# A router joined to the turn ahead of it, with its products per token tile, and the adaptive vectors' weights scaled by ScalarE

## What is computed

```
for layer in range(DEPTH):
    shift_m, scale_m, gate_m, shift_f, scale_f, gate_f = adaln(c, ada_w[layer], ada_b[layer])
    h = rmsnorm(x, norm_mix[layer]) * (1.0 + scale_m) + shift_m
    ...
    h = rmsnorm(x, norm_ffn[layer]) * (1.0 + scale_f) + shift_f
    x = x + gate_f * grouped_moe(h, router_w, router_b, moe_w_gate[layer], moe_w_up[layer], moe_w_down[layer])

def grouped_moe(h, ...):          # 16 experts in 4 groups, 256 tokens
    aff = sigmoid(xf @ router_w)
    biased = (aff + router_b).reshape(T, N_GROUPS, EXPERTS_PER_GROUP)
    grp_score = sum(top_k(biased, 2)); g_sel = argmax(grp_score)
    local = top_k(biased[tok, g_sel], 2)
    w = aff[tok, expert] / sum(...)
    # each token through its two experts (SwiGLU, hidden 512), summed with w
```

## Time and profile before

| | |
|---|---|
| median of 3 runs | 2317.37 us (2312.05 to 2318.6) |
| the profiled execution | 2318.01 us, its span 2316.2 us |
| TensorE, busy | 2108.3 us, 91% of the span |
| VectorE, busy | 1591.7 us, 69% |
| ScalarE, busy | 983.3 us, 42% |
| GpSimd, busy | 709.8 us, 31% |
| mean granted clock of TensorE | 0.937 of full speed |

### The profile page before, as it was taken

How to read it: one execution, slowest core, us unless ns; L and a number is a source line. 1 busy time by engine, 2 the same in 40 slices (tenths; PEclk the granted TensorE clock), 3 DMA queues, 4 the chain that set the end, 5 groups by cost and what they waited for, 6 DMA issues and landing times.

```text
span 2316.2 us, 30766 instructions
## 1 busy us (share of the span) xinstructions
PE 2108.3 (91%) x13090; PEld 1824.9 (79%) x13090; DVE 1591.7 (69%) x1308; ACT 983.3 (42%) x1069; POOL 709.8 (31%) x353
## 2 busy tenths in 40 slices
PE   7998887999899899699989977999998986999997
PEld 6897876999899898699978666877776874877775
DVE  5798536899899774699953556666666247656665
ACT  4433445433433354443333434554453234444553
POOL 2899200899599500089920000000000000000000
PEclk9999898999999899799989987999998787999999
DMA  9886522787678554278754105778986203688874
GB/s 328 272 270 227 183 91 85 261 269 257 230 263 268 174 170 146 95 264 269 246 186 146 55 10 194 278 287 325 341 293 220 82 1 127 226 315 330 310 293 178
DMA packets 224568, 495.95 MB, mean 214 GB/s; under 512 B 11816, under 2 KB 167576, under 8 KB 199696
## 3 DMA queue, kind: packets, MB, share of 16 engines
q1 hardware_dynamic: 200608, 410.20, 51.3%
q0 software_dynamic: 23552, 82.75, 10.4%
q10 hardware_dynamic: 272, 1.05, 0.1%
HBM read 486.57 MB, written 12.10 MB: 215 GB/s over the span
## 4 chain that ended last, share of the span: by engine, by line
PE 82%; DVE 11%; ACT 3%; issue 2%; DMA 2%; DVEq 0%; SPq 0%; ACTq 0%
PE psum L971 79%; DVE nrm L1978 2%; DVE low L1978 2%; DMA ring<-in_ffn_w_up 2%; PE psum L1031 1%; PE psum L1544 1%; PE psum L1198 1%; ACT wh L1633 1%; DVE hl L1978 1%; DVE wide L1978 0%; DVE xl L1978 0%; DVE aux L1978 0%; DVE nrm L2044 0%; DVE nrm L2052 0%; DVE nrm L2042 0%
## 5 line engine op out<-in xcount | busy, mean ns | idle before, releaser
L1978 DVE TENSOR_TENSOR low<-ring,wh 128x2048 fp32r<-128x2048 f32 (+2 forms) x338 | 967.7, 2889 | 350.1 <-ACT wh L1633 349.6
L1633 ACT ACTIVATE wh<-ring 128x2048 fp32r<-128x2048 f32 (+2 forms) x338 | 641.1, 1904 | 616.6 <-PE psum L971 327.1
L971 PE MATMUL psum<-xh,wh 128*128 128x256 f32 x1832 | 521.5, 285 | 8.4 <-DVE low L1978 4.8
L971 PE MATMUL psum<-xl,wh 128*128 128x256 f32 x1832 | 520.3, 284 | 0.0
L971 PE MATMUL psum<-xh,low 128*128 128x256 f32 x1832 | 518.2, 283 | 0.0
L742 POOL TENSOR_TENSOR big<-big 128x1024 f32<-128x1024 f32 x144 | 376.4, 2614 | 11.3
L971 PEld LDWEIGHTS psum<-xh,wh 128*128 128x128 f32 x1832 | 352.7, 193 | 14.2 <-issue 7.9
L971 PEld LDWEIGHTS psum<-xl,wh 128*128 128x128 f32 x1832 | 350.9, 192 | 1.5
L971 PEld LDWEIGHTS psum<-xh,low 128*128 128x128 f32 x1832 | 351.1, 192 | 0.0
L971 PE MATMUL psum<-wh,xh 128*128 128x256 f32 (+5 forms) x864 | 279.0, 323 | 12.5 <-DVEq L645 5.9
L971 PE MATMUL psum<-wh,xl 128*128 128x256 f32 (+5 forms) x864 | 278.2, 322 | 0.0
(11 more groups left out here) (338 smaller groups left out, 2463.4 us busy)
## 6 DMA issues: line engine op xcount, KB each, us to landing
ring<-in_moe_w_gate SPq DMA_DIRECT2D x64, 1024.0 KB, 5.6
ring<-in_moe_w_up SPq DMA_DIRECT2D x64, 1024.0 KB, 6.2
ring<-in_moe_w_down SPq DMA_DIRECT2D x64, 1024.0 KB, 5.8
big<-in_ada_w POOLq DMA_DIRECT2D x48, 1024.0 KB, 7.6
ring<-in_ffn_w_gate SPq DMA_DIRECT2D x44, 1024.0 KB, 5.4
ring<-in_ffn_w_up SPq DMA_DIRECT2D x44, 1024.0 KB, 5.6
ring<-in_ffn_w_down SPq DMA_DIRECT2D x44, 1024.0 KB, 5.9
ring<-in_mlstm_w_in SPq DMA_DIRECT2D x16, 1024.0 KB, 5.6
```

What stands on the lines that cost most here:

```text
L971: return pe.matmul(out_, lhsT, rhs, start=start, stop=stop, **kw)
L1633: act.activation(wh[n % PARTS][:, 0:w], ring[SLOT_OF[n]][:, 0:w], ACT.Copy).then_inc(high, 1)
L1978: return dve.tensor_tensor(out_, a, b, op)
```

## The change

**Adaptive vectors.** ScalarE takes the multiplication by c over: after the down piece's high half of chunks 1 to 8 it waits for the load of one or two pieces (`ADA_PIECES`), and scales each with eight operations of 128x256, one for each column of c (`scale_ada`). GpSimd waits for that (`ada_scaled`) where it waited for the load, and only adds.

**Turn and router.** The pair joins `JOINED`. The router's products are done per token tile: those of tile 0 in the turn, after the wait for the second normed tile and before its transposes, those of tile 1 in the router. ScalarE's copy of the token rows moves into the turn, for tile 0 after its first two copies, for tile 1 after the last two and after a small Sigmoid that brings the table in.

**Ranks and slots.** The comparisons of the three rank computations are two whole operations each instead of eight quarters; one bias addition instead of two; the one-hot of windows 0 and 1 is made first, and the gather of part 0 waits only for it.

**Start of the experts.** The first piece's high and low halves are made right after the first gather copy, and the first expert's gate product waits for the gather copies one by one.

```diff
@@ -228,6 +228,7 @@
         ada_bias_in = sem("ada_bias_in")
+        ada_scaled = sem("ada_scaled")
         ada_step = sem("ada_step")
...
@@ -626,12 +627,13 @@
+        ADA_PIECES = {1: (0,), 2: (1, 2), 3: (3,), 4: (4, 5), 5: (6,), 6: (7, 8), 7: (9,), 8: (10, 11)}
         ADA_TURNS = {0: [(0, 0)], 1: [(0, 3)], 2: [(1, 0)], 3: [(1, 3)]}
         JOINED = [s > 0 and (name, STAGES[s - 1][0]) in (("norm", "residual"), ("final", "residual"),
-                                                         ("turn", "norm"), ("ffn", "turn"), ("project", "turn"), ("moe", "router"),
+                                                         ("turn", "norm"), ("ffn", "turn"), ("project", "turn"), ("moe", "router"), ("router", "turn"),
                                                          ("latent", "project"),
...
@@ -750,17 +752,16 @@
                         pool.wait_ge(ada_out, 16 * (q - 1))
-                    pool.wait_ge(ada_in[j % 2], 32 * q0 + 16 * (j // 2 + 1))
-                    piece, n = ada_w[j % 2], 17 * q + 4 * r
-                    step(n + 1, piece, piece, spread(ccol[:, :], 2, 256), ALU.mult)
-                    step(n + 2, piece[:, 0:4], piece[:, 0:4], piece[:, 4:8], ALU.add)
-                    step(n + 3, piece[:, 0:2], piece[:, 0:2], piece[:, 2:4], ALU.add)
-                    step(n + 4, total[:, 256 * r:256 * r + 256], piece[:, 0], piece[:, 1], ALU.add)
+                    pool.wait_ge(ada_scaled, 4 * q + r + 1)
+                    piece, n = ada_w[j % 2], 13 * q + 3 * r
+                    step(n + 1, piece[:, 0:4], piece[:, 0:4], piece[:, 4:8], ALU.add)
+                    step(n + 2, piece[:, 0:2], piece[:, 0:2], piece[:, 2:4], ALU.add)
+                    step(n + 3, total[:, 256 * r:256 * r + 256], piece[:, 0], piece[:, 1], ALU.add)
                     if j + 2 < rounds:
...
                         pool.wait_ge(ada_bias_in, 16 * (q + 1))
-                        step(17 * q + 17, total[0:1, :], total[0:1, :], ada_bias, ALU.add)
+                        step(13 * q + 13, total[0:1, :], total[0:1, :], ada_bias, ALU.add)
                         pool.dma_start(modpart[layer][first + turn], total).then_inc(ada_out, 16)
...
@@ -1026,10 +1027,22 @@
                         pe.wait_ge(normed, 2 * ran(s, "norm") - 2 + t + 1)
+                    if q == 2 and STAGES[s + 1][0] == "router":
+                        route_products(k, 0)
                     for i in range(4):
...
+            def route_products(turn_, t):
...
+                tokens = slice(t * P, (t + 1) * P)
+                for kt in range(KT):
+                    if kt % 4 == 0:
+                        pe.wait_ge(turn_low, 4 * turn_ + 2 * t + kt // 4 + 1)
+                    last = three(psum[0:E, 0, tokens], both((rw_high, rw_low), slice(0, P), slice(E * kt, E * kt + E)),
+                                 both(xs, slice(0, P), kt, tokens), kt == 0, kt == KT - 1)
+                return last
             def ffn(s, k, chunks):
...
@@ -1396,10 +1409,7 @@
             def router(s, k):
-                for kt in range(KT):
-                    last = three(psum[0:E, 0, 0:T], both((rw_high, rw_low), slice(0, P), slice(E * kt, E * kt + E)),
-                                 both(xs, slice(0, P), kt, slice(0, T)), kt == 0, kt == KT - 1)
-                last.then_inc(route_pe, 1)
+                route_products(ran(s, "turn") - 1, 1).then_inc(route_pe, 1)
                 pe.wait_ge(route_act, k + 1)
...
@@ -1423,7 +1433,7 @@
                     pe.wait_ge(rows_low, 2 * k + 2)
-                    pe.wait_ge(slots_set, 4 * k + 4)
+                pe.wait_ge(slots_set, 6 * k + 2 * part + 2)
                 for j, bank in enumerate(banks):
...
@@ -1439,6 +1449,7 @@
             def weights_of_slots(k):
+                pe.wait_ge(slots_set, 6 * k + 6)
                 for w in range(WINDOWS):
...
@@ -1459,9 +1470,7 @@
                                 if half == 0 and which == "g":
-                                    if q == 0:
-                                        pe.wait_ge(gather_low, 8 * k + 4)
-                                    elif q == 1:
+                                    if q == 1:
                                         pe.wait_ge(gather_low, 8 * k + 8)
...
@@ -1475,6 +1484,8 @@
                                     kt = i + half * KT // 2
+                                    if q == 0 and which == "g" and w == 0 and i % 2 == 0:
+                                        pe.wait_ge(gather_low, 8 * k + kt // 2 + 1)
                                     if w < 4:
...
@@ -1663,6 +1674,16 @@
                                    psum[:, q, :].rearrange("p (a b) -> p a b", a=4), ACT.Copy).then_inc(turn_high, 1)
+                    if STAGES[s + 1][0] == "router" and q % 2:
+                        token_rows(s, q // 2)
...
+            def token_rows(s, t):
...
+                if t == 1:
+                    link(act.activation(stat[:, 7:8], const[:, C_EPS:C_EPS + 1], ACT.Sigmoid))
+                act.wait_ge(normed, 2 * ran(s, "norm") - 2 + t + 1)
+                act.activation(rows_h[:, t, :].rearrange("p (k q) -> p k q", k=KT),
+                               nrm[:, t, :].rearrange("p (q k) -> p k q", k=KT), ACT.Copy).then_inc(rows_high, 1)
             def ffn(s, k, chunks):
...
@@ -1687,7 +1708,18 @@
                         exp_of_pads()
+                    if k in ADA_TURNS:
+                        for j in ADA_PIECES.get(c, ()):
+                            scale_ada(3 * k, j)
                 early_highs(s)
...
+            def scale_ada(q0, j):
...
+                act.wait_ge(ada_in[j % 2], 32 * q0 + 16 * (j // 2 + 1))
+                piece = ada_w[j % 2]
+                for kk in range(KT):
+                    ins = act.activation(piece[:, kk, :], piece[:, kk, :], ACT.Copy, scale=ccol[:, kk:kk + 1])
+                ins.then_inc(ada_scaled, 1)
             def early_highs(s):
@@ -1709,6 +1741,8 @@
                             .then_inc(gather_high, 1)
+                        if part == 0 and j == 0:
+                            high_of(0)
                 def silu_of(q):
...
@@ -1740,7 +1774,7 @@
                 gather_copies(0)
-                for m in range(PARTS):
+                for m in range(1, PARTS):
                     high_of(m)
...
@@ -1934,12 +1968,9 @@
             def router(s, k):
-                for t in range(TT):
-                    act.activation(rows_h[:, t, :].rearrange("p (k q) -> p k q", k=KT),
-                                   nrm[:, t, :].rearrange("p (q k) -> p k q", k=KT), ACT.Copy).then_inc(rows_high, 1)
                 act.wait_ge(route_pe, 3 * k + 1)
                 act.activation(route[0:E, R_AFF:R_AFF + T], psum[0:E, 0, 0:T], ACT.Sigmoid).then_inc(route_act, 1)
-                act.activation(stat[:, 7:8], const[:, C_EPS:C_EPS + 1], ACT.Silu)
+                link(act.activation(stat[:, 7:8], const[:, C_EPS:C_EPS + 1], ACT.Silu))
             def final(s, k):
...
@@ -2139,6 +2170,8 @@
                            hi[:, to, :].bitcast(F32), ALU.subtract).then_inc(gather_low, 1)
+                        if part == 0 and j == 0:
+                            low_of(0)
                 def weighted_hidden(q):
...
@@ -2179,7 +2212,6 @@
                 gather_rests(0)
-                low_of(0)
                 dve.wait_ge(slot_weights, k + 1)
...
@@ -2591,17 +2623,15 @@
                 affinity = psum[:, 1, 0:2 * E].rearrange("p (a b) -> p a b", b=4)
-                rb = small[:, S_RB:S_RB + E].rearrange("p (g e) -> p g e", g=4)
-                for t in range(TT):
-                    link(tt(biased_[:, 4 * t:4 * t + 4], affinity[:, 4 * t:4 * t + 4], rb, ALU.add))
+                link(tt(route[:, 64:96].rearrange("p (t e) -> p t e", t=TT),
+                        psum[:, 1, 0:2 * E].rearrange("p (t e) -> p t e", t=TT),
+                        spread(small[:, S_RB:S_RB + E], 1, TT), ALU.add))
                 def ranks(values, n, g_, e_, out_):
-                    for j in range(4):
-                        other = spread(values[:, :, j], 2, 4)
-                        tt(g_[:, :, j, :], values, other, ALU.is_gt)
-                        last = tt(e_[:, :, j, :], values, other, ALU.is_equal)
-                    link(last)
+                    mine, other = spread(values, 2, 4), spread(values, 3, 4)
+                    tt(g_, mine, other, ALU.is_gt)
+                    link(tt(e_, mine, other, ALU.is_equal))
                     link(tt(e_, e_, spread(lower, 1, n), ALU.mult))
...
@@ -2648,9 +2678,11 @@
                                               in1=spread(seat, 2, WINDOWS), op0=ALU.mult, op1=ALU.add))
+                for w in (0, 2):
+                    for t in range(TT):
+                        tt(onehot[:, t, w:w + 2], spread(iota, 1, 2), spread(seats[:, t, w:w + 2], 2, P), ALU.is_equal)\
+                            .then_inc(slots_set, 1)
                 for t in range(TT):
```

(2 more changed lines are left out.)

## The result

The changed kernel takes 2292.37 us (median of four runs, 2292.11 to 2296.82), beside 2316.98 for the kernel before (four runs). The ratio is 0.9909, with an interval of 0.9883 to 0.9935: 24.6 us less, where 18.5 were forecast. The time lies in the range given, and 1 us outside the sum of the forecast's own bounds (23.6 us gained).

A forecast was written before the change was run, and what follows sets the result against it. TensorE was taken to bound the kernel, waiting only in the first FFN stage and the routers. Gains of 12.1 us there and 6.4 us for both routers, 18.5 in all, took 2317.4 to about 2299 us; range 2291 to 2311.

The forecast's parts named there:

- The bound: Whole kernel: TensorE carries it, waiting only in the first FFN stage (12.5 us for low halves) and in the routers.
- The end of the first FFN stage: First FFN stage and residual: relieving GpSimd gains 12.1 us, bounds nothing and 15 us.
- The wait of 6.1 us: End of first FFN stage: TensorE's wait for low halves goes, as GpSimd is idle from about 199 us; 6.1 us.
- Rival (2): First FFN stage: GpSimd's end moves less, the 6.1 and 3.8 us stay, 2309 us; chance 0.11.
- VectorE's lateness at the residual: Behind the first FFN stage: residual started at 228.0 though ScalarE's root was there at 226.0; 1.9 us go.
- the slow product of x and the gain: Behind the first FFN stage: this product took 3.11 us instead of 1.22; 1.9 us go.
- The early wait of 2.24 us: Earlier in the first FFN stage: TensorE's wait follows a hidden rest that GpSimd stretched; 2.2 us go.
- rival (1): FFN stages: ScalarE's queue becomes the bound, late gate high halves stall TensorE in 16 two-piece chunks; 2331 us, chance 0.12.
- Cost zero in all four stages: FFN stages: ScalarE's new load waits cost TensorE nothing, the gate's high half coming up to 5 us later being covered.
- ScalarE's scaling: FFN stages: eight 128x256 operations take 2.6 us a piece (2.5 to 3.4), some 125 us in all.
- The router: Both routers: scores 2.2 us later, experts 1.8 us earlier, clock 1.4 us; 3.2 us gained each, 6.4 for both.
- rival (3): Routers: 128-token products cost as much as 256-token ones or more, no clock gained; about 2308 us, chance 0.14.

The follow-up runs named there:

- ada_first: The kernel before with ScalarE scaling the adaptive weights in the first FFN stage alone, GpSimd multiplying in the other three, router as before: 2304.37 us, ratio 0.9947.
- nojoin: The changed kernel with the turn-router join undone: 24 products on 256 tokens and the rows' copies behind the turn, as before; 2289.34 us, ratio 0.989.
- no_ranks: The changed kernel with the ranks' eight quarter comparisons back in place of the whole ones: 2297.62 us in one run.
- ada_only: The kernel before with the adaptive vectors' part alone (ScalarE scales, GpSimd only adds), router as before: 2301.34 us, ratio 0.9928.

## Why the prediction was right, step by step

**The bound** was read rightly in the main: FFN 1 and 2 gave nothing (ada_first), the first FFN stage and the routers gave nearly the whole. That the fourth stage repeats the second's row was not quite so: a window over 181 us of it in the kernel before has TensorE idle for 0.9 us.

```profile
985.50:1166.50 181.00, 180.13 (x1284) 168.71 (x1283) 173.62 (x66) 67.79 (x47) 164.19 (x66) 1.00 0.79 261
```

That was worth about 0.8 us, which the sum has at nothing.

**The end of the first FFN stage**, forecast 12.1 us. By the start of the first norm's scaling (237.74 us before, 223.04 after), 14.7 us are gained. The terms:
- The wait of 6.1 us is gone, with GpSimd done at 196.1 us (forecast 199) and the cast at 0.43 us. As forecast. Rival (2) is out.
- VectorE's lateness at the residual is gone (2.1 us, counted from the end of the down products; forecast 1.9), and so is the slow product of x and the gain (3.11 to 1.22, 1.9). As forecast.
- I missed two terms. Behind the 6.1 us of idle time the last down products of the kernel before ran at the low clock:

```profile
219.80:223.20 3.40, 3.35 (x8) 2.71 (x9) 3.40 (x2) 0.00 (x0) 3.32 (x2) 0.50 0.03 10
```

  Eight products there took what sixteen take in the changed kernel (209.80 to 213.20, granted clock 1.00). Over the 24 products behind the wait this was 1.8 us: they lag the same products of the changed kernel by 8.0 us at their first and by 9.8 at their last. I took the clock into account behind the router's wait and forgot it here. And the two updates of x at the residual took 1.92 and 1.66 us instead of 1.28: 1.0 us more, the same disturbance by GpSimd in two rows that I had not looked at.
- The early wait of 2.24 us at 88.59 is gone, but a new one took its place:

```profile
93.65 0.36 PE L972 MATMUL psum<-xh,wh 128*128 128x256 f32 x1 [2.30 <-DVE low L2009]
```

  Ahead of it the queues of ScalarE and GpSimd, and VectorE's from 89.4 to 93.4 us, show why:

```profile
84.32 3.31 ACT L1721 ACTIVATE big<-big,ccol 128x256 f32<-128x256 f32 x8 [2.86 <-DMA big<-in_ada_w]
87.54 3.71 ACT L1644 ACTIVATE wh<-ring 128x2048 fp32r<-128x2048 f32 x2
```
```profile
88.92 8.48 POOL L744 TENSOR_TENSOR big<-big 128x1024 f32<-128x1024 f32 x3
```
```profile
89.47 4.03 DVE L2009 TENSOR_TENSOR low<-ring,wh 128x2048 fp32r<-128x2048 f32 x1 [3.69 <-ACT wh L1644]
```

  ScalarE waited 2.86 us for the piece's load and scaled for 3.31 us before it made the gate's high half, and VectorE waited 3.69 us for that. That is rival (1), at one place and small. It is not all: the low half behind it took 4.03 us instead of 2.28, beside GpSimd's additions, so that some 1.75 of the 2.30 us are the old disturbance. 2.2 us that I had counted as won were not. So what I put at "Cost zero in all four stages" holds for three and not for the first.

The wait (6.4 us from product to product, 6.1 of it idle), 1.8, 2.1, 1.9 and 1.0 make 13.2 of the 14.7 us. The changed kernel is 1.6 us ahead at the last product before the wait: 0.98 us at 106.7 gone, 0.5 less at 74.9, 0.1 since the start. So the sum was 2.6 us low although one of its terms, 2.2, did not come: what I had not counted (1.8, 1.0 and those 1.6) outweighed it. That the sum came this near is in part luck.

**ScalarE's scaling** took 3.31 us a piece, forecast 2.6 and bounded at 3.4. One such operation takes 0.495 us (the mean in the changed kernel's page above), not the 0.40 of the row that I took the earlier trace rows, which is of another form, and back to back they start 0.40 us apart: the overlap is there, the size of one was wrong. 157.2 us in all instead of 125. Outside the place above it cost TensorE nothing that the waits show. The waits of 2.7 us "in most chunks" came in the first stage (23.1 us, eight of them), and once in the other three.

The rule of the Trainium skill on the shared access ("SBUF — State Buffer") would have an addition disturb VectorE as much as a multiplication. The changed kernel still shows such rows beside GpSimd's additions (the pair of low halves at 89.47 us took 7.33 instead of 4.6), so the trace agrees that additions disturb too. That they do so as much, it doesn't show: the mean low half went from 2889 ns to 2400, most of the way to the undisturbed 2.28 us, while GpSimd's busy time went only from 709.8 us to 446.4. And it was not quite free, as I wrote it would be: the wait at 93.65 is in good part such a row.

**The router**, forecast 3.2 us each, measured 4.1 (ledger, first router) and 4.4. By its own terms, first router:

| term | forecast | measured |
|---|---|---|
| start on the scores | 2.2 later | 1.75 later |
| scores to order | 1.2 less | 1.43 less |
| order to gather | 1.1 less | 0.93 less |
| gather to first expert product | 1.7 less | 2.07 less |
| first expert product | 1.8 earlier | 2.7 earlier |
| clock behind it | 1.4 | 1.4 |

The second router repeats these rows within 0.1 us only up to the gather; its first expert product stood at 32.7 us in the kernel before, not 32.15.

No term failed; the sum was 0.9 us low because three were a little better than taken. The clock's 1.4 us needed luck: I took it that under 1 us of idle time keeps the clock up, but nojoin and no_ranks start the experts with no wait at all and run at 0.56 and 0.61 behind it. The 128-token products were spaced by 0.107 us at the low clock, 2.5 us for the 24 (the window above), just above the lower bound of 0.104; rival (3) is out. The Trainium skill's page "TensorE: Matmul & The Clock Gate" ("Wait — 56ns, not 53.3ns?") gives 106 to 107 ns there, and the trace agrees. The drain of 1.38 us at a table load (the Trainium skill, "ScalarE: Activation LUTs", "What ACT_TABLE_LOAD costs") did not show: the load at 1383.54 began within 0.02 us of the copies' end, and the next operation began at 1384.84, 0.02 us behind it. By the Trainium skill's page the scores would have started 1.4 us later than they did.

**The whole.** 14.7 + 4.1 + 4.4 are 23.2 us of the 24.6 between the medians, and more than the 21.6 between the two profiled spans. The difference is in the ledger: the changed kernel's profiled execution lost 2.3 us in FFN 1 and 4.1 in the mLSTM stretch, and won 1.2 in FFN 3, 2.4 ahead of the first router and 1.0 ahead of the second. Of these only the 1.2 us of FFN 3 belong to the change (most of it the wait of 0.87 us). That the stages between stay as they are, which the sum takes for granted, was wrong by some us in each single trace, though it nearly cancelled in the medians; that it cancelled there is luck. What it is comes next.

## What the runs showed that I had not expected

**The same work takes several us more or less by where the clock falls.** The mLSTM stretch, between the same two norms, has the same 1145 matmuls in each kernel. Windows of the kernel before, of the changed kernel, and of ada_only, one each:

```profile
791.20:972.70 181.50, 157.75 (x1145) 149.25 (x1145) 111.60 (x163) 84.09 (x125) 3.30 (x7) 0.88 0.44 131
```
```profile
778.80:964.30 185.50, 162.90 (x1145) 153.51 (x1145) 111.77 (x163) 84.21 (x125) 3.31 (x7) 0.85 0.44 128
```
```profile
776.20:957.60 181.40, 157.68 (x1145) 149.18 (x1145) 111.62 (x163) 84.08 (x125) 3.30 (x7) 0.88 0.44 131
```

VectorE's, ScalarE's and GpSimd's busy times agree within 0.2 us; TensorE's differs by 5.2 us, with the granted clock at 0.88, 0.85, 0.88. The mixer ahead of the second router does it with 9 us, changed kernel first and nojoin second:

```profile
1752.20:1900.20 148.00, 127.54 (x757) 109.83 (x756) 62.62 (x106) 47.55 (x103) 5.55 (x10) 0.80 0.19 64
```
```profile
1748.30:1887.70 139.40, 118.32 (x757) 103.81 (x756) 62.61 (x106) 47.44 (x104) 5.56 (x10) 0.87 0.20 68
```

In these stretches TensorE waits often and its granted clock changes between its two levels; what is gained ahead of such a stretch can come back larger or smaller. None of the edits touches them. What sets it off in one execution and not in another I did not find out: that the earlier start shifts it is only argued. The scatter between runs of one kernel goes the same way: of ada_first's eight runs the fastest, 2292.95 us, had a mean granted clock of 0.945, the slowest, 2310.0, one of 0.934. That is why I let the local times decide where two kernels differ by 3 us.

**A table load costs 1.28 us and nothing else** here, at both routers, with operations right before and behind it: 0.02 us lie between the load and each of them.

## What to carry to other kernels

Work taken off an engine that disturbs another pays only where the disturbed one is late in the end: here 12 of 48 multiplications were worth some 15 us and the other 36 under 1, and a chain of rows at a stage's end (cast, rest, low halves, residual, update, first norm) should be priced whole, the low clock behind its idle time included. Before products are moved into a gap, look at which tile's chain ends last and put its turn first: the same join made the scores 1.75 us later with the products ahead of the turn and the table load in the chain, and 1.7 us earlier with the products behind it and the load moved (2.6 and 0.9 us of the difference). And follow the time past the first product that starts earlier: nojoin's 1.5 us were mostly gone eight products on. A new wait in a busy engine's queue is priced by what is queued behind it, and by the spacing of the loads it waits for: one piece in some chunks and two in others cost TensorE one wait of 2.3 us, two in each of six chunks cost 45 us.
